# Products of constants taken out of the beginnings of five attentions

## What is computed

```
first block:
  h = rmsnorm(x) @ w_in                        -> q, k, v for three branches, a conv group
  o_cmp = attention over 31 compressed tokens
  o_sel = attention over selected blocks of 64 (8 of at most 8: causal)
  o_win = attention over the last 256 tokens   (8 heads of 64; bias by distance)
  x += rmsnorm(concat(rmsnorm(g0*o_cmp + g1*o_sel + g2*o_win), rmsnorm(conv)) @ w_out)
  x += rmsnorm(memory_attention(rmsnorm(x), 256 memory rows, 4 heads of 64))
  x += rmsnorm(swiglu(rmsnorm(x)))             (hidden 2816)
second block:
  x += gate * (branch A: band attention, 8 heads of 64; branch B: mLSTM, 4 heads of 128) @ w_out
  x += gate * (mixture of 16384 experts, 16 per head and token chosen)
  out = rmsnorm(x)
```

## Time and profile before

| | |
|---|---|
| median of 3 runs | 2540.87 us (2537.48 to 2545.16) |
| profiled execution, its own time | 2542.93 us |
| its span in the trace | 2540.7 us |
| mean granted TensorE clock | 0.995 |
| PE busy | 2482.4 us (98%) |
| DVE, ACT, POOL busy | 1617.2 (64%), 969.6 (38%), 1300.2 us (51%) |
| records of the products of constants (L2022) | 110, that is 55 products |

### The profile page before, as it was taken

How to read it: one execution, slowest core, us unless ns; L and a number is a source line. 1 busy time by engine, 2 the same in 40 slices (tenths; PEclk the granted TensorE clock), 3 DMA queues, 4 the chain that set the end, 5 groups by cost and what they waited for, 6 DMA issues and landing times.

```text
span 2540.7 us, 32932 instructions
## 1 busy us (share of the span) xinstructions
PE 2482.4 (98%) x12421; PEld 2088.5 (82%) x12421; DVE 1617.2 (64%) x2551; ACT 969.6 (38%) x1572; POOL 1300.2 (51%) x674
## 2 busy tenths in 40 slices
PE   9999999999999999999999999999999999999998
PEld 6876766878786777788789999999999888888886
DVE  2336243766402624322279896999864699999996
ACT  3256455222223334523333333343433333333333
POOL 3630323444454432044434787555578676676662
PEclk9999999999999999999999999999999999999999
DMA  5320212555433222022223898888999899999992
GB/s 211 116 67 1 68 65 75 199 194 179 151 106 108 83 75 67 26 92 93 98 83 106 276 302 291 287 300 292 299 347 391 323 365 363 361 368 368 363 363 92
DMA packets 212733, 508.92 MB, mean 200 GB/s; under 512 B 18400, under 2 KB 101344, under 8 KB 212192
## 3 DMA queue, kind: packets, MB, share of 16 engines
q1 hardware_dynamic: 123696, 338.22, 38.1%
q0 software_dynamic: 36864, 134.23, 14.8%
q10 hardware_dynamic: 52016, 34.36, 4.3%
HBM read 454.31 MB, written 52.43 MB: 199 GB/s over the span
## 4 chain that ended last, share of the span: by engine, by line
PE 84%; POOL 4%; DVE 3%; ACT 3%; DMA 3%; issue 2%; SPq 0%; ACTq 0%; DVEq 0%
PE bank L2041 69%; PE bank L2523 3%; POOL weight_split L787 3%; PE bank L2140 3%; DMA ring<-weights 2%; PE bank_and L2041 2%; PE bank_and L2011 2%; PE bank L2022 1%; ACT weight_split L928 1%; PE bank L2130 1%; POOL weight_split L803 1%; PE bank_and L2116 1%; PE bank L2116 1%; PE bank_and L2353 0%; POOL arena L814 0%
## 5 line engine op out<-in xcount | busy, mean ns | idle before, releaser
L2041 PE MATMUL bank<-h_split,weight_split 128*128 128x384 f32 (+1 forms) x5640 | 1154.3, 362 | 22.4 <-POOL weight_split L803 8.6
L2041 PEld LDWEIGHTS bank<-h_split,weight_split 128*128 128x128 f32 x5640 | 1007.6, 188 | 143.1 <-issue 20.2
L787 POOL TENSOR_TENSOR weight_split<-ring,weight_split 128x1024 fp32r<-128x1024 f32 x185 | 464.2, 2509 | 779.0 <-ACT weight_split L928 778.9
L2041 PE MATMUL bank<-late_weight_split,weighted_split 128*128 128x512 f32 x2268 | 514.8, 389 | 0.0
L2041 PEld LDWEIGHTS bank<-late_weight_split,weighted_split 128*128 128x128 f32 x2268 | 425.7, 188 | 88.2
L814 POOL DMA_INDIRECT arena<-weights,arena x256 | 315.0, 1231 | 210.6 <-DVE arena L1798 124.3
L803 POOL TENSOR_TENSOR weight_split<-ring,weight_split 128x1024 fp32r<-128x1024 f32 x129 | 310.0, 2404 | 66.0 <-ACT weight_split L1282 63.5
L928 ACT ACTIVATE weight_split<-ring 128x1024 fp32r<-128x1024 f32 x185 | 195.0, 1054 | 295.0 <-PE bank L2041 278.1
L1282 ACT ACTIVATE weight_split<-ring 128x1024 fp32r<-128x1024 f32 x130 | 137.7, 1060 | 397.4 <-PE bank L2041 294.7
L1939 DVE TENSOR_TENSOR arena<-arena 128x384 f32<-128x384 f32 x128 | 228.8, 1788 | 3.8 <-DMA arena<-expert_acts 3.5
L803 POOL TENSOR_TENSOR late_weight_split<-ring,late_weight_split 128x1024 fp32r<-128x1024 f32 x63 | 152.0, 2412 | 103.6 <-ACT late_weight_split L1282 102.8
(11 more groups left out here) (337 smaller groups left out, 2772.7 us busy)
## 6 DMA issues: line engine op xcount, KB each, us to landing
ring<-weights SPq DMA_DIRECT2D x493, 512.0 KB
expert_acts<-arena SPq DMA_DIRECT2D x128, 192.0 KB
gates_spread<-arena ACTq DMA_DIRECT2D x24, 1024.0 KB
arena<-gates_spread SPq DMA_DIRECT2D x96, 256.0 KB
arena<-expert_acts SPq DMA_DIRECT2D x128, 192.0 KB
arena<-weights,arena POOLq DMA_INDIRECT x256
arena<-bias_sel ACTq DMA_DIRECT2D x1, 2048.0 KB, 7.7
arena<-bias_band ACTq DMA_DIRECT2D x1, 2048.0 KB, 8.1
```

Source lines behind the costliest of these rows:

```text
L787: nc.gpsimd.tensor_tensor(w_split[:, (count - 1) % 2, 1, :], ring[:, n % RING, :], w_split[:, (count - 1) % 2, 0, :], ALU.subtract).then_i ...
L2041: ins = mm(*args, start=start, stop=stop)
```

## The change

The argument `busy` of `attend` and its two calls of `keep_busy` are taken out, and with them the call before the transposes of the compressed attention. Of 55 products of constants 27 go: 6 in the window attention, 4 in the compressed, 4 in the selected, 4 and 3 in the memory and 6 in the band attention. The 28 around the norms stay. Nothing else is added or moved; the lines behind it are up to three lower.

```diff
-            def attend(u0, g0, units, per, q, k, blocks, head, vals, before_turn=None, begun=0, busy=(0, 0)):
+            def attend(u0, g0, units, per, q, k, blocks, head, vals, before_turn=None, begun=0):
...
                             turn_prob(2 * (pair - 1) + half)
-                    if pair < 2:
-                        keep_busy(busy[pair], (3, 5)[pair])
...
-                   before_turn=lambda: pe.wait_ge(*taken(first["vtok"] + 3)), begun=2, busy=(0, 6))
+                   before_turn=lambda: pe.wait_ge(*taken(first["vtok"] + 3)), begun=2)
...
             pe.wait_ge(probT_ready, U_SEL)
-            keep_busy(4, 3)
             for t in range(NT):
...
-                   lambda i, c: nsa_v(i, 0, c), busy=(4, 0))
+                   lambda i, c: nsa_v(i, 0, c))
...
-                   lambda i: i % MH, lambda i, c: mv[:, c, (i % MH) * HD:(i % MH + 1) * HD], busy=(4, 3))
+                   lambda i: i % MH, lambda i, c: mv[:, c, (i % MH) * HD:(i % MH + 1) * HD])
...
-                   before_turn=lambda: pe.wait_ge(full_ready, full_base["yb"] + 4), begun=2, busy=(0, 6))
+                   before_turn=lambda: pe.wait_ge(full_ready, full_base["yb"] + 4), begun=2)
```

## The result

The changed kernel took 2573.18 us (median of 4, 2561.57 to 2577.24) against 2540.57 us: ratio 1.0119, 95% interval 1.0103 to 1.0135 (the recorded ratios are estimated from the single executions and differ a little from the quotient of the medians, 1.0128 here). That is 32.6 us slower. The forecast was 62 us slower; the direction, the cause and the places were right, but the size was about twice too large.

A forecast was written before the change was run, and what follows sets the result against it. PE, busy 98% of the span, was taken as the bound. Low-clock cost of 77.5 us less 15.8 us given back made +61.7 us on 2540.87 us, rounded to 2603 us; 8-in-10 range 2528 to 2642 us.

The forecast's parts named there:

- PE's own order bounds the time, and the products cost what they overshoot the waits by: All six places: removal gives back window 1.4, compressed 0.5, selected 1.7, memory 5.3, band 6.9, together 15.8 us.
- The clock falls at the window, the compressed or selected, and the band attention, not at the memory attention: Opened waits of nearly 4 us (window) and 3 us (compressed) drop the clock; memory's bare waits are under 1 us.
- PE's time doubles at the low clock: In the attentions other engines have room, so at half rate the cost is the length of the stretch.
- How long it stays low: In the attentions the clock stays low until the densest work, the 512-wide units; cost 77.5 us in all.
- the terms for the window and the selected attention: Cost of the low clock: 34 us for the whole window attention, 20.5 us for the selected before its 512-wide units.
- the band attention went as forecast: Band attention at the low clock until its 512-wide units: 20.4 less 1.4, a cost of 19 us.
- The 4 us for the compressed part: Compressed attention: small score products, 3.6 us in all, double at the low clock; the rest hides behind DVE.
- the same sum: Whole kernel: low-clock cost 77.5 us less 15.8 us given back, net +61.7 us.
- at once: Rival: the clock falls but a few microseconds of the attention's steady work restore it; 2530 us, chance 0.25.
- only behind the attentions: Rival: the clock stays low through whole attentions until the dense products behind; 2646 us, or some 2638; chance 0.17.
- half way: Rival: the clock returns in the 256- or 384-wide units, 10 to 14 us per attention; 2561 us, chance 0.13.
- the two rises that I had: Clock rises seen in the kernel before, both behind unbroken full products; used to argue attention work would not restore it.

The follow-up runs named there:

- band_out: Kernel before without only the 6 products of the band attention: 2544.49 us, ratio 1.0024.
- band_early: Kernel before with, in the band attention, 2 products ahead of PE's wait for the last projection and 1 behind, replacing 6 behind: 2536.72 us, ratio 0.9990.
- the repeat: The changed kernel, nothing altered, measured a second time against the kernel before: 2553.25 us, ratio 1.0056.
- window_out: Kernel before without only the 6 products of the window attention: 2548.86 us, ratio 1.0035.
- later: Changed kernel with 6 products put into the fifth step of both window and band attention, where PE waits for nothing: 2554.52 us, ratio 1.0051.
- safer: Against trimmed, more products: 5 window, 4 compressed, 3 selected, band 2 before the last projection's wait and 2 behind: 2528.77 us, ratio 0.9966.
- trim_more: Against trimmed, fewer products: 2 window, 1 compressed, 1 selected, band 1 before the last projection's wait and none behind: 2550.18 us, ratio 1.0039.
- memory_out: Kernel before without only the 7 products of the memory attention: 2537.05 us, ratio 0.9982.
- trimmed: Kernel before with products cut: 4 window, 3 compressed, 2 selected, 0 memory, band 2 before the last projection's wait and 1 behind: 2530.03 us, ratio 0.9965.
- window_kept: Against trimmed, the window attention's 6 products back in full: 2529.63 us, ratio 0.9959.
- selected_kept: Against trimmed, the 4 and 4 products of the compressed and selected attention back in full: 2529.78 us, ratio 0.9977.

## Why the prediction was right and wrong

- *PE's own order bounds the time, and the products cost what they overshoot the waits by.* Right. Window −1.0 (forecast −1.4), memory −5.3 (−5.3, measured by itself). Compressed and selected together came out 1.0 us earlier although the clock was low for 6.8 us there. In `band_out` it took 7.4 us less from the memory attention to the first product with values (forecast −6.9); two other low stretches on that way, 3.4 us less and 3.4 us more than before, cancel.
- *The clock falls at the window, the compressed or selected, and the band attention, not at the memory attention.* Right at each place and in both profiles. The one thing I had not expected is that it came back within the compressed part, at 222.2, and fell again at 229.1, behind a wait of 2.2 us for the first probabilities:

```profile
226.50 0.72 PE L2130 MATMUL bank<-const,arena 128*128 128x128 f32 x2 [2.19 <-ACT arena L940]
```

- *PE's time doubles at the low clock.* Nearly: in the longest case (`band_early`) 46.5 us of the attention at 0.50 did what the kernel before does in 25.7 (38.6 less the 12.9 done at 1.00), a factor of 1.81. Each of these microseconds cost 0.45; the lines through whole executions give mostly 0.4 to 0.5.
- *How long it stays low.* This is the step that failed, and with it the terms for the window and the selected attention: "the whole window attention, 35.7 less about 1.7 for its narrow first pairs, where PE had slack: 34", with 20.5 in the selected. I had it come back only with the 512-wide units. In the window attention, which has none, it was back after 20.5 us, in the repeat and in `window_out` after 10.2, and the cost was 7.7 and 3.9 us; in the selected it was back after 23.9 us of low clock in the 384-wide units, for 10.4 us. In the first profile the band attention went as forecast (back in the 512-wide units, 19.4 us for 19), but that was luck: in the repeat it was back after 27.3 us, in the 384-wide units, for 11.5 us. The 4 us for the compressed part fell away: when its small score products ran, the clock was up again (since 184.7), and they took 3.6 us as before. With the measured 7.7, 10.4 and 19.4 in place of 34, 20.5 and 19, and nothing extra in the compressed part, the same sum gives 37.5 − 15.8 = +21.7 us, near the 18.6 of the profiled execution; the two short low stretches that it lacks, 3.4 us together, nearly make up the difference. Why the clock rises where it does within an attention stays open.
- *The rivals.* The clock came back neither at once nor only behind the attentions. The "half way" case, 10 to 14 us per attention, is what the first profile shows on average: 12.5 us. I gave it 0.13 because I had no row of an attention at 1.2 GHz and took the two rises that I had for typical. Its 2561 us is nearly the time of the profiled execution, but the other three took 2570.9 to 2577.2 us. The Trainium skill's "TensorE: Matmul & The Clock Gate" ("What's actually happening") says that activity releases the throttle. The runs agree, but with an attention's mix of scores, transposes and narrow products at work it took 10 to 48 us; in `later` the clock was back within 4 us of the first full-width product.
- *Size.* +32.6 us in the first measurement and +12.2 in the second, for a forecast of +62. Both are slower by more than the 0.3% (7.6 us) that can be told from no change.

## What to carry to other kernels

Products that nobody reads are worth their time only where PE would wait, and only as long as that wait. Here the kernel without them was 12 to 33 us slower, and the one with them cut to the waits and spread over two neighbouring waits 11 us faster (`safer`, ratio 0.9966, five executions within 8.4 us). The loss is not the wait but what the clock does in the long stretch of narrow work behind it, so look at the granted clock behind each wait of some 2 us, above all where attention follows: in all profiles the falls outside the attentions, the one at the kernel's end aside, were over after 3.4 or 6.8 us, while those in attentions lasted up to 47.8. And take several executions: with the clock at stake one kernel's times spread over 20 us, and a median from one set can sit 20 us from the next.

## What the runs showed of the hardware

- A fall can be short or very long with little or no change in what PE does. One and the same kernel had 20.5 and 10.2 us at 0.50 in the window attention and 44.4 and 27.3 us in the band attention. Over all kernels it was 10.2 to 34.1 us in the window attention and, where it reached into the band attention, 10.2 to 47.8 us (the 10.2 in `later`, with products in it, and in `trim_more`).
- An idle time of 1.93 us stood before a fall of 34.1 us (`trim_more`); behind waits of 0.72 us and 0.78 us (`memory_out`) none was seen. A wait of about 2 us doesn't always bring a fall: at the same place in the products of the memory rows, with the same idle time of 1.85 us, the clock fell in the kernel before (idle from 324.4 us) and not in the changed one (from 340.6 us), and in neither did it fall behind an idle time of 2.12 us (from 1587.9 and 1606.7 us).
- The fall need not lie in the wait: in `trim_more` it came at 168.6 us, behind a wait that had ended at 166.28.
- The kernel before, too, had a low stretch of 6.8 us at the band attention, where six products filled the time until the clock was back. With two ahead of PE's wait and one or two behind, the profiles differ: no low stretch there in `trimmed`, `window_kept` and `selected_kept`, 3.4 us in `safer`, 47.8 us in `band_early`.
